# Attention: VectorE scales the probabilities of the step ahead before it reads this step's scores

## The reference, cut to what matters

```python
sc = jnp.einsum('blhd,bmhd->bhlm', qc, kb) * scale + bias
sc = jnp.where(valid, sc, -jnp.inf)
p = jax.nn.softmax(sc, axis=-1)
return jnp.einsum('bhlm,bmhd->blhd', p, vb)
```

## Time and profile before

| what | value |
|---|---|
| median of three runs | 2040.19 us (2036.47 to 2045.55) |
| the profiled execution's own time | 2045.85 us |
| its span | 2044.1 us |
| busy share of the span | PE 96%, DVE 37%, ACT 31%, POOL 29% |
| the attention's loop | from 613.7 us (first scores) to 795 us |
| from 613.7 to 786 us: PE busy | 148.36 of 172.30 us |
| from 786 to 795 us: PE busy | 6.30 of 9.00 us |
| TensorE's granted clock (1.00 is full speed) | 0.50 from within 616 to 617 us to within 640 to 641 us, then 1.00 to 786 us |

### The profile page before, as it was taken

The page is one execution under the profiler, slowest core; times in us unless marked ns, Lnnn a source line. Parts: engine busy times, 40 slices in busy tenths (PEclk is TensorE's granted clock), DMA queues, the critical chain, the costliest instruction groups (busy, mean ns, idle before and its releaser), DMA issues. The chain is left out here.

```text
span 2044.1 us, 34231 instructions
## 1 busy us (share of the span) xinstructions
PE 1954.5 (96%) x14050; PEld 1767.8 (86%) x14050; DVE 747.8 (37%) x1478; ACT 634.3 (31%) x1238; POOL 590.0 (29%) x456
## 2 busy tenths in 40 slices
PE   7999999999998888899799999999999999999998
PEld 7899999999984566687699879999999999999996
DVE  5211777111125654555554182222222222222225
ACT  5101222100015664344353245222222222222222
POOL 3111111112221002543254244333333333333333
PEclk9999999999997998999799999999999999999999
DMA  4322223522226313031153332111111111111123
GB/s 118 102 93 87 76 87 128 197 88 97 89 93 215 104 63 84 27 113 39 33 170 119 104 124 83 42 44 50 43 42 42 42 42 42 42 42 42 46 76 147
DMA packets 159273, 169.22 MB, mean 83 GB/s; under 512 B 14187, under 2 KB 130043, under 8 KB 159150
## 3 DMA queue, kind: packets, MB, share of 16 engines
q1 hardware_dynamic: 152814, 141.52, 22.5%
q10 hardware_dynamic: 6336, 25.96, 3.2%
HBM read 126.84 MB, written 40.55 MB: 82 GB/s over the span
## 5 line engine op out<-in xcount | busy, mean ns | idle before, releaser
L2330 DVE TENSOR_TENSOR t_acc<-t_acc,t_B 128x512 f32<-128x512 f32 x252 | 173.4, 688 | 540.7 <-PE t_B L2423 540.7
L116 PE MATMUL i_ps<-x_hi,i_w_lo 128*128 128x384 f32 x1008 | 337.4, 335 | 0.0
L116 PE MATMUL i_ps<-x_hi,i_w_hi 128*128 128x384 f32 x1008 | 337.4, 335 | 0.0
L116 PE MATMUL i_ps<-x_lo,i_w_hi 128*128 128x384 f32 x1008 | 337.3, 335 | 0.0
L2410 PE MATMUL t_B<-t_merged_hi,t_wm_lo 128*128 128x384 f32 x768 | 256.9, 335 | 1.0 <-POOL t_wm_lo L2035 1.0
L2410 PE MATMUL t_B<-t_merged_lo,t_wm_hi 128*128 128x384 f32 x768 | 256.6, 334 | 0.0
L2410 PE MATMUL t_B<-t_merged_hi,t_wm_hi 128*128 128x384 f32 x768 | 256.6, 334 | 0.0
L106 POOL TENSOR_TENSOR i_w_lo<-i_w_raw,i_w_hi 128x1024 fp32r<-128x1024 f32 x44 | 105.3, 2394 | 433.6 <-ACT i_w_hi L101 433.6
L2035 POOL TENSOR_TENSOR t_wm_lo<-t_raw,t_wm_hi 128x1024 fp32r<-128x1024 f32 x49 | 119.0, 2428 | 295.6 <-ACT t_wm_hi L2110 295.6
L116 PEld LDWEIGHTS i_ps<-x_hi,i_w_lo 128*128 128x128 f32 x1008 | 189.8, 188 | 0.0
L116 PEld LDWEIGHTS i_ps<-x_lo,i_w_hi 128*128 128x128 f32 x1008 | 189.7, 188 | 0.0
(11 more groups left out here) (338 smaller groups left out, 3475.8 us busy)
## 6 DMA issues: line engine op xcount, KB each, us to landing
proj<-i_out ACTq DMA_DIRECT2D x44, 576.0 KB, 2.8
i_w_raw<-in_w_in SPq DMA_DIRECT2D x44, 512.0 KB, 3.9
t_raw<-in_w_up SPq DMA_DIRECT2D x32, 512.0 KB, 4.2
t_raw<-in_w_down SPq DMA_DIRECT2D x32, 512.0 KB, 3.6
t_gates<-proj SPq DMA_DIRECT2D x48, 192.0 KB, 2.6
a_k_cache<-in_cache_attn_k SPq DMA_DIRECT2D x8, 1024.0 KB, 5.2
a_v_cache<-in_cache_attn_v SPq DMA_DIRECT2D x8, 1024.0 KB, 5.3
d_c<-proj SPq DMA_DIRECT2D x3, 1536.0 KB, 8.4
```

What stands on the lines that cost most here:

```text
L116: last = pe.matmul(out, a[s][:, c, :], b[:, c, tokens], start=k == 0, stop=k == n - 1)
L2330: dve.tensor_tensor(a, a, B[(ND * j + d) % 4][:, :], ALU.add).then_inc(added, 1)
```

## The change

In each step of its loop DVE now scales unit st - 1 first, and only then reads the scores of this step; the copies of the queries and of O keep their places behind the reading. No instruction is added, removed or altered, and each keeps its waits.

```diff
             for st in range(STEPS):
+                u = st - 1
+                if 0 <= u < NU:
+                    recip(u)
                 if st < NU and (st % STEP % 2 == 0 or not prompt(st)):
                     soft(st)
                     if prompt(st):
...
                 u = st - 6
                 if 0 <= u < NU and (u % STEP % 2 or not prompt(u)):
                     out(u)
-                u = st - 1
-                if 0 <= u < NU:
-                    recip(u)
```

## The result

The changed kernel took 2044.54 us in the median of 12 runs (2039.75 to 2049.26), the kernel before 2039.91 us in 12 runs beside it (2034.64 to 2045.55). The ratio is 1.0022 with a 95% interval from 1.0013 to 1.0032: 4.5 us slower, between 2.7 and 6.5. The forecast was 2.2 us.

What follows compares the result with a forecast made beforehand. PE was taken to bound the kernel, busy 96% of the span. The terms 1.30 + 0.44 + 0.5 + 0 = 2.2 us, added to the median of 2040.2, gave 2042.4 us, range 2035 to 2050.

Steps and rivals of the forecast that it cites:

- What bounds it, and that the scaling brought forward gains nothing: Whole kernel: PE bounds it, busy 96% of the span; it waits for the scaled probabilities only once, 0.7 us.
- the faster rival: PE's transposes were waiting for the scaling after all: up to 11.2 us less, 2029 us; chance 0.04.
- The price of a scaling ahead of a reading: In DVE's queue: the reading starts no earlier than 0.70 us after the previous unit's exponential ends.
- Blocks of 640 keys, 0: Blocks 4 to 7: the later readings stay hidden from PE, cost 0; 0.4 to 1.2 us if margins are misread.
- The room in a pair's step: Blocks 4 to 7, step that begins a pair: the reading could start 0.31 us before its scores let it.
- The slower rival (every step): The reading waits for the exponential at every step, 0.4 us late 39 times: 15.6 us more, 2056; chance 0.07.
- The boundaries: Into blocks 1, 2 and 3: late readings delay the copy of O and PE's values product, together 1.30 us.
- Block 0, 0.44 and 0.5: Block 0, 128 keys: 0.44 us for a scaling before the second pair's reading, 0.5 for a multiplication beside POOL's copy.
- The 0.5 us for the multiplication caught by POOL's copy: Block 0: a scaling falling behind the start of POOL's bias copy delays two readings; 0 to 1.4 us, taken as 0.5.
- The clock: Rival: a low-clock stretch near blocks 0 and 1 vanishes, 2034 us, or a second appears, 2050; chance 0.10, half each side.
- the sum of 2.2: Whole kernel: boundaries 1.30, block 0's 0.44 and 0.5, blocks 4 to 7 0; 2.2 us slower in all.
- The signs named in advance: Profile after: blocks 1 and 2 grow 0.3 to 0.6 us, attention 1 to 4, everything after keeps its length.

Runs made afterwards that it cites:

- e1: Against the kernel before, the scaling ahead of the reading only from the second step of block 4 on; 2041.14 us for 2039.77, ratio 1.0007.
- e3: Against the kernel before, the scaling ahead of the reading in all steps but the first of each block; 2044.33 us for 2040.34, ratio 1.0017.
- e4: As the changed kernel, but the copy of O first in each step; 2034.50 us against 2040.34 of the kernel before, ratio 0.9965.
- e6: Against the kernel before, the scaling ahead of the reading in block 0 alone; 2042.10 us for 2039.77, ratio 1.0015.
- e10: A third profile of the changed kernel, nothing else altered; blocks 0 and 1 together took 36.07 us.
- e5: As the kernel before, scaling last, but the copy of O first in each step; 2032.81 us for 2040.34, ratio 0.9960.
- e2: Against the kernel before, the scaling ahead of the reading only up to the first step of block 4; 2044.70 us for 2040.34, ratio 1.0012.
- e7: Against the kernel before, the scaling ahead of the reading in all blocks but block 0; 2043.90 us for 2039.77, ratio 1.0019.

## Why the prediction was right, and where it fell short

What is shown of the 4.5 us is the part of the order. At equal clock it is 1.9 and 2.2 us (0.4 each), and the profiles have 1.8 of it in places: block 0 0.29, from 0 into 1 0.31, blocks 2 and 3 0.64 and 0.43 (means of three profiles each), blocks 4 to 7 0.1. The other 2.3 us or so go with the lower mean clock of the runs. Of these the start of the delta rule has 1.3 (17.2 and 18.5 us, means of three). Where the rest lies is not shown: blocks 0 and 1 are 2.2 us longer in the changed kernel's profiles (means 34.2 and 36.4), the order's 0.6 among them, but the six profiled executions differ by only 3.1 us in all (means 2042.6 and 2045.7): elsewhere, around 1010 us above all, before stays longer at the lower level.

- *What bounds it, and that the scaling brought forward gains nothing*: right. PE's waits for the transposes' copy are the same 10.5 us, and the 0.7 for the scaling stays; the faster rival falls.
- *The price of a scaling ahead of a reading, 0.70 us after the exponential*: 0.69 and 0.70 in the two timelines above.
- *Blocks of 640 keys, 0*: right, 0.02 us in blocks 5 and 6 and 0.06 in block 4; e1 shows it alone. The room in a pair's step, 0.31 predicted, is 0.22. DVE's idle time in the pair's step lies on both sides of the scaling now. The slower rival (every step) falls.
- *The boundaries*: predicted 0.62 and 0.39 us for blocks 2 and 3, measured 0.64 and 0.43. From 0 into 1 predicted 0.29: the values product there comes at 630.46 in both profiles, 2.41 us after the block's first scores (628.05) before and 2.72 after them (627.74) now: 0.31. The mechanism was the one named, the copy of O behind a late reading, and e3 and e4 take it away in two ways.
- *Block 0, 0.44 and 0.5*: too much. By the profiles shown block 0 is 0.29 us longer, 14.64 us for 14.35, with PE waiting for ACT's copy of the cached keys as predicted; e6 found nothing at equal clock (-0.1, 0.4), which does not exclude 0.3. The 0.5 us for the multiplication caught by POOL's copy was 0 in two of the three profiles, where it started 0.28 and 0.24 us ahead of that copy, and 0.42 in e10, where it came 0.19 behind its start (a wait of 0.94 us for 0.52). Which of the two happens hangs on some tenths of a microsecond.
- *The clock*: this is the term that was missing from the sum. I had it as a rival with as much chance of a gain as of a loss, priced at 0.15 to 0.5 us for each us at the lower level. The price was right (1.09 us for 0.001 of the mean, which over 2040 us is 4.1 us at the lower level: 0.27), the sign was not even: every kernel with the scaling brought forward in early blocks had a mean clock of 0.983, and that goes with about 2.3 us more (0.0021 of mean clock). Why it goes with a lower clock stays open. So the sum of 2.2 was right for the order of the queue, 1.9 and 2.2 at equal clock in two sets of runs, and half of what was measured. That it fits so closely is partly luck: block 0's 0.94 was too high, and the parts found in the profiles come to 1.8.
- *The signs named in advance*: the attention grew by 2.9 us in the profiles shown (182.5 to 185.3), within the 1 to 4. That everything after it keeps its length was wrong: the start of the delta rule grew. And 1 to 4 us for the whole was missed by the 4.5 of the runs, though not by their interval.

## What to carry to other kernels

A queue in order has room only as long as its dearest wait is shorter than what the next engine has still to do; here that failed where short first blocks have one long unit among them, so work out the boundary and not only the steady state. An instruction that frees a single buffer (here the copy of O) is worth trying ahead of everything that waits for something newer: moving it brought 8 us, four times what the change cost at equal clock. And where two kernels differ by some tenths of a per cent, compare them at equal mean clock too, and state both: here the lower clock came with the change each time, and an account by stretches of a few profiles did not explain it.

## What the runs showed that was not expected

- PE's waits before the stream's values product, laid to ACT in the waits, were for DVE's copy of O: 7.3 us in 7 waits in the kernel before, gone in e5.
- Bringing the scaling forward in the first four blocks, or in part of them, came with a mean granted clock of 0.983 instead of 0.985 over the whole execution in six sets of 10 to 12 runs (e2, e3, e6, e7 and the change twice), while e1, changed only later, kept 0.985. The 9 runs of e4 have 0.983 too, the 7 of e5 0.984. In the profiles only the start of the delta rule, with some 3.5 us more at the lower level, goes with the early change throughout, and e4 lacks it.
- The multiplication beside POOL's copy, which the prediction put at 0.5 us between bounds of 0 and 1.4, was caught in one profiled execution of the changed kernel and missed in two.
